# A fused decoder-layer kernel: the retention stage's loads, weight splits and first unit in another order

## What is computed

```
h = x @ w_in
qa, ka, va, za, qr, kr, vr, zr, ga, gb = split(h)
o_a = dilated_mixture_attention(qa, cached + new keys, cached + new values)
qr = rotary(qr); kr = rotary(kr) * R_KEY_DIM ** -0.5
per head and chunk of 128:
    att = (q @ k.T) * dmat
    o   = att @ v + (q @ S) * q_decay
    S   = chunk_decay * S + (k * k_decay).T @ v
y_a = (silu(za) * o_a) @ w_pa;  y_b = (silu(zr) * groupnorm(o_r)) @ w_pb
out = (sigmoid(ga) * y_a + sigmoid(gb) * y_b) @ w_o
y = layernorm(alpha * x + out)
```

## Time and profile before

| | us |
|---|---|
| median of three runs | 1173.52 (1172.69 to 1173.59) |
| span of the profiled execution | 1171.8 |
| PE busy | 1059.9 (90%) |
| DVE busy | 572.4 (49%) |
| ACT busy | 365.3 (31%) |
| POOL busy | 138.8 (12%) |
| DMA | 219.46 MB, mean 187 GB/s |

### The profile page before, as it was taken

How to read it: one execution, slowest core, us unless ns; L and a number is a source line. 1 busy time by engine, 2 the same in 40 slices (tenths; PEclk the granted TensorE clock), 3 DMA queues, 4 the chain that set the end, 5 groups by cost and what they waited for, 6 DMA issues and landing times.

```text
span 1171.8 us, 22131 instructions
## 1 busy us (share of the span) xinstructions
PE 1059.9 (90%) x8036; PEld 960.9 (82%) x8036; DVE 572.4 (49%) x1105; ACT 365.3 (31%) x524; POOL 138.8 (12%) x144
## 2 busy tenths in 40 slices
PE   5999999999999969896988698869988999999893
PEld 5999999999999969573967396738764999999893
DVE  3245335335434536665576556554657532332328
ACT  3133124213413422233323332433133443243100
POOL 0101011010100102103030303030302100000003
PEclk8999999999999989997999899998999899999997
DMA  8767575665666444346433633454153788888512
GB/s 280 244 215 271 190 244 193 205 213 202 214 216 236 169 161 146 117 135 213 138 132 123 225 118 100 175 178 165 44 196 107 263 278 263 266 276 273 189 37 81
DMA packets 136377, 219.46 MB, mean 187 GB/s; under 512 B 7680, under 2 KB 102016, under 8 KB 134464
## 3 DMA queue, kind: packets, MB, share of 16 engines
q1 hardware_dynamic: 131744, 205.38, 52.0%
q0 software_dynamic: 3920, 10.89, 2.8%
q10 hardware_dynamic: 656, 2.36, 0.5%
HBM read 206.01 MB, written 99.88 MB: 261 GB/s over the span
## 4 chain that ended last, share of the span: by engine, by line
PE 78%; DVE 7%; issue 7%; DMA 3%; ACT 2%; POOL 1%; SPq 1%; DVEq 0%; POOLq 0%; ACTq 0%
PE bank L630 19%; PE bank L631 19%; PE bank L632 19%; PE bank L625 7%; PE bank L843 4%; DMA cslot<-in_cache_kv_w_dram 2%; PE bank L704 2%; PE bank L726 2%; DVE part_l L1399 2%; PE bank L980 1%; PE bank L879 1%; PE bank L859 1%; DMA xn<-in_x_prompt_dram 1%; PE bank L884 1%; ACT part_h L1142 1%
## 5 line engine op out<-in xcount | busy, mean ns | idle before, releaser
L630 PE MATMUL bank<-wh,xh 128*128 128x256 f32 x800 | 235.7, 295 | 10.6 <-DVE vr L1485 7.5
L631 PE MATMUL bank<-wl,xh 128*128 128x256 f32 x800 | 230.1, 288 | 2.5 <-issue 2.5
L632 PE MATMUL bank<-wh,xl 128*128 128x256 f32 x800 | 229.9, 287 | 0.0
L630 PE MATMUL bank<-xh,wh 128*128 128x288 f32 x640 | 193.2, 302 | 2.0 <-POOL wl L606 2.0
L632 PE MATMUL bank<-xh,wl 128*128 128x288 f32 x640 | 189.3, 296 | 0.0
L631 PE MATMUL bank<-xl,wh 128*128 128x288 f32 x640 | 189.3, 296 | 0.0
L630 PEld LDWEIGHTS bank<-wh,xh 128*128 128x128 f32 x800 | 157.6, 197 | 13.9 <-DVE vr L1485 8.8
L632 PEld LDWEIGHTS bank<-wh,xl 128*128 128x128 f32 x800 | 157.2, 197 | 2.6 <-issue 2.6
L631 PEld LDWEIGHTS bank<-wl,xh 128*128 128x128 f32 x800 | 157.6, 197 | 0.6
L1215 DVE TENSOR_TENSOR wl<-raw,wh 128x1024 fp32r<-128x1024 f32 (+1 forms) x96 | 109.2, 1175 | 38.6 <-ACT wh L1046 27.7
L1046 ACT ACTIVATE wh<-raw 128x1024 fp32r<-128x1024 f32 (+1 forms) x104 | 101.2, 1016 | 85.3 <-PE bank L632 79.0
(11 more groups left out here) (185 smaller groups left out, 1708.7 us busy)
## 6 DMA issues: line engine op xcount, KB each, us to landing
cslot<-in_cache_kv_w_dram SPq DMA_DIRECT2D x48, 1024.0 KB, 5.9
out_dram<-in_cache_kv_w_dram SPq DMA_DIRECT2D x20, 2040.0 KB, 10.5
raw<-in_w_in_dram SPq DMA_DIRECT2D x128, 256.0 KB
out_dram<-in_cache_kv_w_dram SPq DMA_DIRECT2D x24, 1020.0 KB, 9.6
out_dram<-in_cache_kv_w_dram SPq DMA_DIRECT2D x20, 504.0 KB, 5.4
raw<-in_w_in_dram SPq DMA_DIRECT2D x16, 512.0 KB
out_dram<-in_cache_kv_w_dram SPq DMA_DIRECT2D x24, 252.0 KB, 3.3
out_dram<-kv POOLq DMA_DIRECT2D x16, 256.0 KB, 3.0
```

Of the source, the lines that this page charges most:

```text
L630: pe.matmul(out, lhs[0](k), rhs[0](k), start=(k == 0), stop=False)
L631: pe.matmul(out, lhs[0](k), rhs[1](k), start=False, stop=False)
L632: last = pe.matmul(out, lhs[1](k), rhs[0](k), start=False, stop=(k == n - 1))
```

## The change

SP issues each head's first key tiles before it waits for the states of the head before (keys 2r + 2 behind values 2r + 1; the first head's before the end of stage A). The wait on `states_out` now stands ahead of the value weights. The next head's query/key weights are loaded in mid-head, behind values 2r, and the states behind keys 2r + 1. The tile slots lie behind the other tiles of stage B in SBUF, beyond what stage A uses. ACT makes the high part of the value weights before its first value tiles, and that of the next query/key weights behind them, when unit 4 is done. POOL makes their low part right after `kd`. PE computes unit 0 behind the scores. DVE copies unit 0 after `rows(0)`, and splits the value weights after `probs(0)`, ahead of `projected(2)`.

```
-        cslot = [sb(f"cslot{s}", ...)]
+        cslot = [sb(f"cslot{s}", ...)]
@@ SP
-            sp.wait_ge(a_end, 4)
             def stage_b(r, last):
-                keys(r * 2)
+                sp.wait_ge(states_out, r + 1)
                 retention_chunk(r * B_CH + (C0_B + 1), r, 1)
                 values(r * 2)
-                sp.wait_ge(w_low, r * (2 * B_CH) + (2 * C0_B + 6))
-                sp.dma_start(st[:, :, :], state_ret...).then_inc(st_in, 16)
-                keys(r * 2 + 1)
-                values(r * 2 + 1)
-                sp.wait_ge(states_out, r + 2)
                 if last:
                     gate_chunk(C0_C, 0)
                 else:
                     retention_chunk(r * B_CH + (C0_B + 2), r + 1, 0)
+                keys(r * 2 + 1)
+                sp.wait_ge(w_low, r * (2 * B_CH) + (2 * C0_B + 8))
+                settle(sp)
+                sp.dma_start(st[:, :, :], state_ret...).then_inc(st_in, 16)
+                values(r * 2 + 1)
+                if not last:
+                    keys(r * 2 + 2)
+            keys(0)
+            sp.wait_ge(a_end, 4)
             with sp.Fori(0, RH - 1) as r:
                 stage_b(r, False)
             stage_b(RH - 1, True)
+            sp.wait_ge(states_out, RH + 1)
@@ POOL
                 tt(kd[:, :, :], rot[:, :, RK:2 * RK], kdec, ALU.mult).then_inc(kd_done, 1)
+                pool.wait_ge(w_low, r * (2 * B_CH) + (2 * C0_B + 6))
+                for s in range(2):
+                    pool.wait_ge(w_high, r * (2 * B_CH) + (2 * C0_B + 4 + s + 1))
+                    tt(wl[0][:, s * HW:(s + 1) * HW], wraw[s], wh[0][...], ALU.subtract).then_inc(w_low, 1)
 ...
                 pool.sem_inc(states_out, 1)
-                for s in range(2):
-                    pool.wait_ge(w_high, r * (2 * B_CH) + (2 * C0_B + 4 + s + 1))
-                    tt(wl[0][:, s * HW:(s + 1) * HW], wraw[s], wh[0][...], ALU.subtract).then_inc(w_low, 1)
@@ PE
+                cached_scores(0)
                 chunk_ready(r * B_CH + C0_B)
-                natural(0, unit(0), 0, 0)
-                cached_scores(0)
-                for t in range(1, TT):
-                    if t == 3:
+                for t in range(TT):
+                    if t == 2:
                         cached_probs(0)
                     natural(0, unit(t), t, t % 2)
@@ ACT
                 rows(0)
+                high(r * B_CH + (C0_B + 1), 1, used_b(0))
                 values(0, 0, 3)
-                high(r * B_CH + (C0_B + 1), 1, used_b(0))
+                high(r * B_CH + (C0_B + 2), 0, used_b(5))
 ...
                 output_lows(1)
-                high(r * B_CH + (C0_B + 2), 0, used_b(5))
@@ DVE
                 queries(0)
-                projected(0)
                 lows(0, 0, 2, TILES, [(7, lambda: queries_4_to_7(0))])
                 rows(0)
+                projected(0)
+                normalise_rows(0)
                 projected(1)
-                normalise_rows(0)
-                projected(2)
                 probs(0)
-                projected(3)
                 dve.wait_ge(w_low, r * (2 * B_CH) + (2 * C0_B + 4))
                 settle(dve)
                 low(r * B_CH + (C0_B + 1), 1)
-                projected(4)
+                for t in (2, 3, 4):
+                    projected(t)
                 values(0)
```

More of the change, by code:

```diff
@@ L244, in bass_hybrid_step @@
         scope_b = ExitStack()
-        cslot = [sb(f"cslot{s}", [P, n, H * DH], F32, scope_b) for s, n in enumerate((5, 4, 4))]
         part_h = [sb(f"part_h{b}", [P, H * P], F32R, scope_b) for b in range(3)]
@@ L274, in bass_hybrid_step @@
         half = sb("half", [P, TT], F32, scope_b)
+        cslot = [sb(f"cslot{s}", [P, n, H * DH], F32, scope_b) for s, n in enumerate((5, 4, 4))]
         scope_b.close()
@@ L461, in stage_b @@
             def stage_b(r, last):
-                keys(r * 2)
+                sp.wait_ge(states_out, r + 1)
                 retention_chunk(r * B_CH + (C0_B + 1), r, 1)
                 values(r * 2)
-                sp.wait_ge(w_low, r * (2 * B_CH) + (2 * C0_B + 6))
-                sp.dma_start(st[:, :, :], state_ret[:, bass.ds(r, 1), :, :].rearrange("b r d e -> d (b r) e"))\
-                    .then_inc(st_in, 16)
-                keys(r * 2 + 1)
-                values(r * 2 + 1)
-                sp.wait_ge(states_out, r + 2)
                 if last:
@@ L475, in stage_b @@
                     retention_chunk(r * B_CH + (C0_B + 2), r + 1, 0)
+                keys(r * 2 + 1)
+                sp.wait_ge(w_low, r * (2 * B_CH) + (2 * C0_B + 8))
+                settle(sp)
+                sp.dma_start(st[:, :, :], state_ret[:, bass.ds(r, 1), :, :].rearrange("b r d e -> d (b r) e"))\
+                    .then_inc(st_in, 16)
+                values(r * 2 + 1)
[3 more added lines that the diff above has]
+            sp.wait_ge(a_end, 4)
             with sp.Fori(0, RH - 1) as r:
@@ L578, in _ @@
                 tt(kd[:, :, :], rot[:, :, RK:2 * RK], kdec, ALU.mult).then_inc(kd_done, 1)
+                pool.wait_ge(w_low, r * (2 * B_CH) + (2 * C0_B + 6))
+                for s in range(2):
+                    pool.wait_ge(w_high, r * (2 * B_CH) + (2 * C0_B + 4 + s + 1))
+                    tt(wl[0][:, s * HW:(s + 1) * HW], wraw[s], wh[0][:, s * HW:(s + 1) * HW].bitcast(F32),
+                       ALU.subtract).then_inc(w_low, 1)
                 pool.wait_ge(kd_done, r + 2)
@@ L603, in _ @@
                 pool.sem_inc(states_out, 1)
-                for s in range(2):
-                    pool.wait_ge(w_high, r * (2 * B_CH) + (2 * C0_B + 4 + s + 1))
-                    tt(wl[0][:, s * HW:(s + 1) * HW], wraw[s], wh[0][:, s * HW:(s + 1) * HW].bitcast(F32),
-                       ALU.subtract).then_inc(w_low, 1)
             own.leave(RH)
```

## The result

Four executions of the changed kernel took 1196.83 us (1196.25 to 1197.52), four of the kernel before beside them 1173.55 (1172.69 to 1176.03): the ratio is 1.0195 [1.0177, 1.0214]. The forecast said slower, 1178.4, but its range ended at 1184. The profiled execution's span grew from 1171.8 to 1195.8 us, and that is what has to be explained: +24.0 where +4.9 had been worked out.

The account below looks back on a forecast made before the run. TensorE carried 78% of the chain of waits, so its idle gaps were what could be won. Gains 15.8 + 1.2 = 17.0 against cost 21.9 gave 1173.5 + 4.9 = 1178.4 us, range 1159 to 1184.

Parts of the forecast that it names:

- last work of a stage or head to first score: Four head starts: 52.4 us falls to 19.8, taking 4.3 at three boundaries and 6.9 for the first head.
- slow clock on the scores: After the boundary gap the slow clock falls on the score matmuls: some 1.2 us a head, 4.8 in four.
- collision: Behind kd, GpSimd's subtractions take turns with VectorE's value subtractions, delaying the last value unit: 15.9 us in four heads.
- last unit's clock: Last value unit runs at half clock after PE's idle time: 1.5 us more a head, 6.0 in all.
- end of the stage: Retention stage's end: the 2.00 us wait for GpSimd's subtraction goes, but only 1.2 us are kept.
- The boundary is a matter of transfers: Head boundaries: PE's 7.04, 6.86, 5.83 and 6.13 us before the first key tile were put down to late loads.
- loop: Head boundary: 0.15 us allowed within the 4.3 us from PE's last work to its first score.
- over exactly this work: Unit 0 had lain over the tile split and query work before the first score; moving it saves nothing, 12.0 us reappear.
- B: Value units: GpSimd's request loses to VectorE once, so the last unit is delayed less; 1166.5 us, chance 0.15.
- C: Value units: no collision at all, for instance because GpSimd's subtraction becomes ready after VectorE's three; 1156.5 us, chance 0.15.
- Rival D: Boundary: key tiles still land late, gain about 5 us, time 1190; sign an idle stretch before first transposes; chance 0.07.
- Part 3's other costs: Mid-head weights: ACT's splits, the weight load and SP's later second keys and state load were each put at cost 0.

Follow-up runs that it names:

- subtractions later and unit 0 back: Changed kernel, PE's loop kept, with GpSimd's two subtractions behind the masked key product km and unit 0 ahead of the scores again: 1159.15 us, ratio 0.9864.
- subtractions later: Changed kernel with GpSimd's two subtractions moved from behind kd to behind the masked key product km: 1175.21 us, ratio 1.0012.

## Why the prediction was off

With the loop kept, the runs split the change as follows (us, medians):

| part | runs compared | us |
|---|---|---|
| early key tiles, weights mid-head, GpSimd off the head's end | subtractions later and unit 0 back, against before | -14.8 |
| unit 0 behind the scores | subtractions later, against that | +16.1 |
| GpSimd's subtractions behind kd | the change, against subtractions later | +21.6 |
| sum | | +22.9 |

Measured directly, the change is +23.3; the 0.4 between is the scatter of the sets.

The forecast's own sum, part by part, in the profiled executions:

| part | forecast | measured |
|---|---|---|
| last work of a stage or head to first score (52.4 before) | 19.8, so -32.6 | 37.4, so -15.0 |
| first score to last value unit but one: unit 0, slow clock on the scores | +12.0 + 4.8 = +16.8 | +16.9 |
| from there to the rotation's transposes: collision, last unit's clock | +21.9 | +23.0 |
| end of the stage | -1.2 | -0.9 |
| net | +4.9 | +24.0 |

The measured column is from PE's timeline: the second line is 3.8, 4.4, 4.9 and 3.8 us in the four heads (before each took 37.3 us), the third is 50.0 us against 26.9. The four lines add up to the 24.0 by which the span grew, so the rest is unmoved in sum. One line is wrong, the first.

**The step that failed is the sentence "The boundary is a matter of transfers".** I took all four gaps before the first key tile for a wait on the tiles, and set the gap to 0.15 us ("loop") once they were early, with no row behind that number. Only the first head's row says DMA; the other three say "issue", time in which PE waited for nothing that the profile shows. The full DMA engines beside them were no proof. The chain of waits of the kernel before, read piece by piece (start, us, what), had even said so:
```profile
536.01 7.78 DMA cslot<-in_cache_kv_w_dram
543.80 6.36 issue
550.16 1.94 PE bank L625 x8
```
The tile had landed at 543.80, 0.5 us after PE's last work, and PE stood for another 6.36; at the next two boundaries another 4.62 and 4.00. After the change the tiles land 7 us early (second head) and the gap is 4.36, 3.74 and 4.61 us; with the loop written out it is gone, in both kernels; with a shorter body and the loop kept it is 0.17. What ended last at the boundary was the fetch of PE's own instructions behind the branch back, and not a transfer of data. So of the 17.6 us by which the boundary was mis-sized, 12.3 are these three gaps (12.7 less 0.15 each), and 4.3 the way from the first transpose to the first score, 5.6 us at the second boundary (551.40 to 556.98) where 4.15 was assumed: the transposes behind a gap run at half clock (0.50 from 551 to 560), and ACT, DVE and the queries come behind them. The last 1.0 us is the first head's (7.93 against 6.9).

**Unit 0.** The sum named what it covered ("over exactly this work") and counted its loss, but it took the loss for one that the closed gap repays. The gap didn't close, and where it is closed, with the loop written out, unit 0 behind the scores still costs 13.6 us. Moving it cost 11.2 us on the kernel before and 16.1 on the changed one (with the later subtractions): it is a loss in all three.

**The collision** was right in mechanism, place and size: GpSimd's instruction behind kd, VectorE's value subtractions taking turns with it (longest 2867 ns, forecast 2.9 us), the last unit delayed by 3.0 us in the first head (forecast 3.3) and 4.2 in the second (4.6), half clock behind it. The total of 23.0 against 21.9 flatters the two terms: the four delays are 14.6 us, not 15.9, and the slow clock on the last units is 8.4 us, not 6.0, and the misses have opposite signs. Rivals B and C are out: both of GpSimd's instructions found a VectorE subtraction to wait with (three took 7.14 us), and the kernel without the collision is 21.6 us faster.

**Rival D** came nearest in size (1190), with the wrong reason, so its nearness is luck. It asked for late tiles; they were early. The idle stretch that I had named as its sign is there, under "issue".

**Part 3's other costs** were nothing, as assumed: no wait for weights shows in the value units or at unit 4. **Part 4** kept 0.9 of 2.0 us.

**What stays open.** How much of a loop body the engine keeps isn't settled. The retention body has 770 matmuls, as many weight loads, and the waits, and is fetched again each turn; with 184 matmuls and their weight loads less it isn't; nor is that of the attention stage, which has 774 matmuls a turn, gaps of 0.2 us at its turns and no instruction transfer from 107 to 432 us. I tried one shorter body only, and ran it once. Why the gaps differ is half answered by the traces. The same two parts of the gap in the kernel before:
```profile
543.30:547.30 4.00, 0.00 (x1) 0.00 (x0) 0.27 (x2) 0.42 (x1) 2.90 (x2) 0.55 1.05 399
547.30:550.16 2.86, 0.00 (x1) 0.03 (x1) 0.00 (x0) 0.00 (x0) 0.00 (x0) 0.50 1.07 359
```
The part behind the packet is as long beside full DMA engines (2.86 us, share 1.07) as beside empty ones (2.73 us, share 0.04). What differs is how late the packet comes: 3.0 to 4.1 us after PE's last work in the two kernels with late tiles, 0.9 to 2.6 in the five with early ones. That it queues behind the data transfers fits, but wasn't tried by itself.

## What to carry to other kernels

A gap at the first instruction of a loop's turn that the profile puts under "issue" need not be a late transfer of data, however busy the DMA engines look beside it: ask whether its input had landed, look for packets of the instruction queue in the gap, and try the loop written out before reordering any loads. Work that stands between a producer chain and its consumer (here unit 0 between the transposes and the scores) is cover; move it only when the chain is gone. And put a long GpSimd instruction where VectorE works from PSUM or waits, not beside a run of two-input SBUF subtractions that frees a PE bank.

## What the runs showed of the hardware

**Fetch behind a branch.** At each of the three returns of PE's four-turn loop the engine stood still for 3.7 to 4.6 us in the changed kernel, 5 us and more after its tiles had landed. Of this 2.7 to 2.8 us lie behind the packet of the instruction queue, beside nearly empty DMA engines (share 0.04 to 0.17). Writing the loop out gave 18.3 us on the kernel before, 17.6 on the changed one and 19.6 on the one with the later subtractions. In the changed kernel that is more than the gaps themselves (12.7). Part of the rest is the clock: from the first transpose to the first score of the second head the granted clock was 0.50 and the stretch took 5.58 us; written out, it was 0.59 and 4.73 us. The Trainium skill, "Runtime: NRT & Kernel Launch", section "Instruction fetch mechanics", says that a taken branch whose target isn't in the current window of two pages forces a fetch of that page before execution goes on. The trace agrees as to the stall, with 4.36 us for it, but not as to the window of two pages. By the same section a page is 256 instructions, and the short body, with 586 matmuls and as many weight loads a turn, came back three times without a transfer; here the measurement decides. The section also gives PE room for 2048 instructions. By that, the nine transfers of a head are an estimate of up to 2304 instructions, which wouldn't fit; the matmuls and weight loads that the trace shows are 1540, and how many instructions without a record stand beside them no run here shows.

**Turns on the shared port.** Three VectorE subtractions of 0.68 us beside two GpSimd ones of 2.35 took 7.14 us, and GpSimd's 2.80 each: 3 x 0.68 + 2 x 2.35 = 6.7, so they ran nearly one after another. With GpSimd's in halves, the same work in four instructions, the same three took 4.99. The lock for a whole instruction, weighed in the prediction, is what both runs show.

**The clock behind a gap.** After 4.25 us without matmuls PE's next unit ran at 0.50 throughout (5.3 us for 24 matmuls against 3.0). A stall of 2.1 us takes the clock in some heads only: in the kernel with the later subtractions, where it stands before the last unit but one, the two last units take 6.1 us in the first and third head and 7.3 in the second and fourth.
